# Expert rows moved by id, and a ring slot reloaded in two parts, in a two-layer decoder step

## The reference

```python
def hierarchical_moe(h, rg_w, rg_b, re_w, re_b, w_gate, w_up, w_down):
    x = h.reshape(-1, d)
    gp, gidx = lax.top_k(softmax(x @ rg_w + rg_b), 1)          # one of 4 groups
    sel = take_along_axis((x @ re_w + re_b).reshape(-1, 4, 8), gidx)
    ew, eidx = lax.top_k(softmax(sel), 2)                      # two of its 8 experts
    hid = silu(einsum("nd,edf->nef", x, w_gate)) * einsum("nd,edf->nef", x, w_up)
    out = einsum("nef,efd->nd", hid * gate[:, :, None], w_down)
```

## Time and profile before

| what | value |
|---|---|
| device time, median of 3 runs | 1407.9 us (1406.41 to 1408.34) |
| device time of the profiled execution | 1405.64 us |
| its span, first to last instruction | 1403.9 us |
| PE busy | 1036.7 us, 74% |
| DVE busy | 695.8 us, 50% |
| ACT busy | 326.8 us, 23% |
| POOL busy | 227.7 us, 16% |
| moved by DMA | 305.14 MB, mean 217 GB/s |

### The profile page before, as it was taken

One profiled execution on the slowest core, in us unless ns is written; L12 is line 12 of the kernel. 1 busy time (PEld: TensorE's weight loads), 2 busy tenths in 40 slices (PEclk: granted clock), 3 DMA queues, 4 the chain that ended last, 5 costly groups with the idle time before them and its releaser, 6 DMA issues.

```text
span 1403.9 us, 17270 instructions
## 1 busy us (share of the span) xinstructions
PE 1036.7 (74%) x5203; PEld 631.5 (45%) x5203; DVE 695.8 (50%) x1284; ACT 326.8 (23%) x430; POOL 227.7 (16%) x215
## 2 busy tenths in 40 slices
PE   5999999917767777742769999369927777799850
PEld 4999974413222222221668998235423222233320
DVE  2323324352333333339299999934452333355438
ACT  2222110004333332232210110040004322243330
POOL 3333310020000000022337645000020000000020
PEclk8999999958899998875789999679957989899985
DMA  9475220295999999971130110000195999999943
GB/s 307 142 291 206 76 93 0 80 373 199 388 395 393 398 385 373 382 244 52 59 120 1 61 58 34 7 4 0 55 380 177 391 397 391 389 359 367 371 157 138
DMA packets 78220, 305.14 MB, mean 217 GB/s; under 512 B 13243, under 2 KB 31727, under 8 KB 53583
## 3 DMA queue, kind: packets, MB, share of 16 engines
q1 hardware_dynamic: 56248, 235.16, 44.5%
q10 hardware_dynamic: 16295, 49.76, 10.3%
q0 software_dynamic: 5632, 19.63, 3.9%
HBM read 270.76 MB, written 46.27 MB: 226 GB/s over the span
## 4 chain that ended last, share of the span: by engine, by line
PE 36%; DMA 26%; DVE 23%; issue 5%; SPq 5%; ACT 2%; POOL 2%; ACTq 1%; DVEq 0%; PEldq 0%
DMA ring<-in_moe_w_down_dram 23%; DVE ring L1486 13%; PE ps L881 13%; PE ps L901 10%; PE ps L972 6%; PE ps L987 3%; SPq L408 2%; DMA ring<-in_sc_w_in_dram 1%; POOL rows_sorted L837 1%; PE ps L913 1%; PE ps L958 1%; DVE bn L1172 1%; DVE h L1182 1%; DVE h L1390 1%; DVE h L1392 1%
## 5 line engine op out<-in xcount | busy, mean ns | idle before, releaser
L972 PE MATMUL ps<-arena 128*64 128x512 f32 x1152 | 287.7, 657 | 95.6 <-DVE arena L1349 93.2
L972 PEld LDWEIGHTS ps<-arena 128*64 128x64 f32 x1152 | 88.7, 151 | 291.8 <-issue 161.7
L1486 DVE SCALAR_TENSOR_TENSOR ring<-arena,cvec,ring 128x528 f32<-128x528 f32 x360 | 189.5, 605 | 0.0
L1348 DVE COPY arena<-ring 128x1024 f32 x144 | 99.4, 690 | 168.6 <-SPq L474 146.0
L881 PE MATMUL ps<-hT_hi,w_hi 128*128 128x296 f32 x640 | 145.0, 308 | 33.3 <-POOL w_lo L801 12.6
L901 PE MATMUL ps<-ring 128*128 128x512 f32 (+1 forms) x320 | 140.4, 598 | 11.9 <-ACT ring L750 11.9
L987 PE MATMUL ps<-arena 128*64 128x512 f32 x576 | 131.5, 598 | 21.2 <-DVE arena L1365 21.2
L801 POOL TENSOR_TENSOR w_lo<-ring,w_hi 128x512 fp32r<-128x512 f32 x80 | 109.5, 1371 | 203.8 <-ACT w_hi L538 203.8
L881 PE MATMUL ps<-hT_lo,w_hi 128*128 128x296 f32 x640 | 141.0, 302 | 0.0
L881 PE MATMUL ps<-hT_hi,w_lo 128*128 128x296 f32 x640 | 140.7, 301 | 0.0
L881 PEld LDWEIGHTS ps<-hT_hi,w_hi 128*128 128x128 f32 x640 | 105.0, 192 | 40.9 <-issue 30.0
(11 more groups left out here) (194 smaller groups left out, 962.7 us busy)
## 6 DMA issues: line engine op xcount, KB each, us to landing
ring<-in_moe_w_gate_dram SPq DMA_DIRECT2D x64, 1024.0 KB, 10.2
ring<-in_moe_w_up_dram SPq DMA_DIRECT2D x64, 1024.0 KB, 12.6
ring<-in_moe_w_down_dram SPq DMA_DIRECT2D x64, 1024.0 KB, 14.8
arena<-rows_sorted ACTq DMA_DIRECT2D x160, 128.0 KB
rows_sorted<-arena ACTq DMA_DIRECT2D x144, 128.0 KB
rows_sorted<-stage ACTq DMA_DIRECT2D x27, 512.0 KB, 3.6
ring<-in_sc_w_in_dram SPq DMA_DIRECT2D x12, 1024.0 KB, 12.7
ring<-in_cf_w_pw_dram SPq DMA_DIRECT2D x4, 1536.0 KB, 15.1
```

The costliest lines, as they stand in the source:

```text
L972: ins = nc.tensor.matmul(ps[own, B_GU, :], xT_e[:, k, own], w_gu[:, x, c, i * 2 * F:(i + 1) * 2 * F], start=(k == 0), stop=(k == C - 1))
L1348: nc.vector.tensor_copy(as_gu(w_gu[:, 0, c, :]), gu_chunk(ranks[0], c))
L1486: ins = nc.vector.scalar_tensor_tensor(out=out, in0=src, scalar=cf_tap(k, j), in1=out, op0=ALU.mult, op1=ALU.add)
```

## The change

Rows no longer pass through a sorted array. As each tile of `h` leaves the first LayerNorm, ACT stores it to `x_dram`, in the order of the rows. `route` makes, from the places, the inverse table: with one-hot matrices of each pair's place (its low 7 bits in `r_low`, its duo in `r_high` times the pair's number) PE adds up which pair sits at each place (`ids_turned`), and DVE makes of it the row numbers to gather (`xidx`) and the pair numbers to scatter to (`yidx`); an empty place gets a number beyond the bound, which the DMA leaves out. For each duo POOL then gathers 128 places' rows from `x_dram` and scatters 128 results to `y_dram` with one indirect DMA each. `y_dram` is in the order of the pairs, so that ACT can fetch a tile's two results per row with one plain DMA; `picked` has a buffer for each of the five tiles. The zero fill, the ten scatters, the ten gathers, the pieces and their flags in `tab` go. ACT's down copies of duo 0 come first in its part, before it waits for any row. The last duo stands outside the loops of PE and ACT.

SP waits for `gu_ready` alone before the gate and up DMAs, and for `dn_ready` before the down DMA; it reads the expert's number ahead of both waits.

```diff
-            def load_expert(layer, r, number=None):
+            def load_expert(layer, r, number=None, duos=None):
...
+                down = w_down[layer, e1].rearrange("e (p k) d -> p (e k d)", k=FK)
+                if duos is not None:
+                    sp.wait_ge(gu_ready[layer], NCH * duos + 1)
...
-                                 (s[:, 2 * u:3 * u], w_down[layer, e1].rearrange("e (p k) d -> p (e k d)", k=FK))):
+                                 (s[:, 2 * u:3 * u], down)):
+                    if duos is not None and src is down:
+                        sp.wait_ge(dn_ready[layer], FK * duos + 1)
                     sp.dma_start(dst, src, **cond).then_inc(slot_loaded[r % SLOTS], 16)
...
-                        wait_copied(layer, upto)
-                        load_expert(layer, r, g * SLOTS + r)
+                        load_expert(layer, r, g * SLOTS + r, (upto + 1) // 2)
...
-                def body(s, first=False):
+                def body(s, first=False, final=False):
-                    rank_a, rank_b, y_a, y_b, x_a, x_b = record(mybir.EngineType.Activation, s, 0, 6)
-                    copy_dn(s, (rank_a, rank_b), first)
                     if not first:
-                        store_y(s - 1, (y_a, y_b))
+                        copy_dn(s, record(mybir.EngineType.Activation, s), first)
                     act.wait_ge(gu_used[l], NCH * s + NCH)
...
-                    copy_xT(s + 1)
-                    load_x(s + 2, (x_a, x_b))
+                    if not final:
+                        copy_xT(s + 1)
 
                 act.sem_inc(dn_ready[l], 1)
-                act.wait_ge(scattered, 16 * 2 * NT * (l + 1))
...
-                load_x(0, flags[0:2])
-                copy_xT(0)
-                load_x(1, flags[2:4])
+                copy_dn(0, record(mybir.EngineType.Activation, 0), True)
+                act.wait_ge(x_stored, 16 * NT * (l + 1))
                 for t in range(2):
                     scale_h(t, h_scaled)
+                copy_xT(0)
                 body(0, first=True)
-                with act.Fori(1, last + 1) as s:
-                    body(s)
-                store_y(last, record(mybir.EngineType.Activation, last + 1, 2, 2))
                 for t in range(2, NT):
                     scale_h(t, h_scaled)
-                act.wait_ge(x_loaded[l], (last + 3) * MOVED)
-                act.wait_ge(y_stored[l], (last + 1) * MOVED)
...
+                with act.Fori(1, last) as s:
+                    body(s)
+                body(last, final=True)
+                act.wait_ge(y_stored[l], (last + 1) * 16)
+                for t in range(NT):
+                    n = ROWS[t]
+                    act.dma_start(picked[t][0:n, :], y_dram[2 * t * P:2 * (t * P + n), :].rearrange("(p c) d -> p (c d)", c=2)
+                                  ).then_inc(y_fetched[t], 16)
...
-                if p.index >= 3:
-                    store_blanks(p.index - 3)
...
                     if t >= 1:
                         copy_hT((i + 1) * NT + t - 1)
+                        act.wait_ge(ln_done, i * NT + t)
+                        n = ROWS[t - 1]
+                        act.dma_start(x_dram[(t - 1) * P:(t - 1) * P + n, :], h[0:n, t - 1, :]).then_inc(x_stored, 16)
...
+            def experts(l):
+                pool.wait_ge(tab_ready, l + 1)
+                last = last_duo(pool)
+                x_bound, y_bound = pool.to_reg(T - 1), pool.to_reg(PAIRS - 1)
+                def at_column(i, column, s):
+                    nc.gpsimd.tensor_copy(now[:, i:i + 1], column[:, bass.ds(s, 1)])
+                    pool.drain()
+                    return bass.IndirectOffsetOnAxis(ap=now[:, i:i + 1], axis=0)
+                def load_x(s):
+                    pool.indirect_dma_start(x_rows, None, x_dram[:], at_column(0, xidx, s), bounds_check=x_bound,
+                                            oob_is_err=False).then_inc(x_loaded[l], 16)
+                def store_y(s):
+                    pool.wait_ge(y_copied[l], s + 1)
+                    pool.indirect_dma_start(y_dram[:], at_column(1, yidx, s), y_rows, None, bounds_check=y_bound,
+                                            oob_is_err=False).then_inc(y_stored[l], 16)
+                pool.wait_ge(x_stored, 16 * NT * (l + 1))
+                load_x(0)
+                pool.wait_ge(x_turned[l], 1)
+                load_x(1)
+                with pool.Fori(0, last - 1) as s:
+                    pool.wait_ge(x_turned[l], s + 2)
+                    load_x(s + 2)
+                    store_y(s)
+                store_y(last - 1)
+                store_y(last)
...
-                pool.wait_ge(pos_ready, layer + 1)
...
-                pool.wait_ge(ys_complete, layer + 1)
...
+                experts(layer)
...
+                pe.wait_ge(places_ready, layer + 1)
+                for i in range(2 * NT):
+                    last = nc.tensor.matmul(ps[:, B_IDS, 0:NDUO], r_low[:, i, :], r_high[:, i, :],
+                                            start=(i == 0), stop=(i == 2 * NT - 1))
+                last.then_inc(ids_turned, 1)
...
+                nc.vector.tensor_scalar(posh[:, 0], posi[:], P - 1, None, ALU.bitwise_and)
+                step(nc.vector.tensor_scalar(posh[:, 1], posi[:], P.bit_length() - 1, 1, ALU.logical_shift_right,
+                                             ALU.logical_shift_left))
+                step(nc.vector.tensor_copy(poshf[:], posh[:]))
+                step(tt(r_high, evens[:].unsqueeze(1).to_broadcast([P, 2 * NT, NDUO]),
+                        poshf[:, 1].unsqueeze(2).to_broadcast([P, 2 * NT, NDUO]), ALU.is_equal))
+                step(tt(r_high, r_high, ids[:].rearrange("p c t -> p (c t)").unsqueeze(2).to_broadcast([P, 2 * NT, NDUO]),
+                        ALU.mult))
+                tt(r_low, iota_n[:].unsqueeze(1).to_broadcast([P, 2 * NT, P]),
+                   poshf[:, 0].unsqueeze(2).to_broadcast([P, 2 * NT, P]), ALU.is_equal).then_inc(places_ready, 1)
...
-                nc.vector.memset(x_rows, 0.0)
...
+                dve.wait_ge(ids_turned, layer + 1)
+                found = ps[:, B_IDS, 0:NDUO]
+                step(nc.vector.tensor_scalar(idt[:], found, 0.5, blank[:, 0:1], ALU.is_lt, ALU.mult))
+                step(nc.vector.scalar_tensor_tensor(out=yidx[:], in0=found, scalar=-1.0, in1=idt[:], op0=ALU.add, op1=ALU.add))
+                nc.vector.tensor_scalar(xidx[:], yidx[:], 1, None, ALU.logical_shift_right).then_inc(ids_ready, 1)
```

More of the change, by code:

```diff
@@ L51, in build_decoder_step @@
     NDUO = -(-TILES // 2)
-    XROWS = (NDUO + 2) * P
     CAP = -(-T // R)
@@ L189, in build_decoder_step @@
         hidT = hidT.rearrange("p (k n) -> p k n", k=FK)
-        picked = [v[:, 2 * D * b:2 * D * (b + 1)].rearrange("p (k d) -> p k d", k=2)
-                  for v in (mixT[:].rearrange("p c t -> p (c t)"), work) for b in range(2)]
-        NB = len(picked)
+        tail = ring[:, SHARED * SLOT:SHARED * SLOT + 6 * D]
+        picked = [tail[:, 2 * D * b:2 * D * (b + 1)] for b in range(3)] + [work[:, 2 * D * b:2 * D * (b + 1)] for b in range(2)]
+        assert len(picked) == NT and C * T + DIAGS * P + C * SB >= 6 * D
         r_e = work[:, 0:6 * NT * EG].rearrange("p (i t e) -> p i t e", t=NT, e=EG)
@@ L277, in build_decoder_step @@
         y_stored = [sem(f"y_stored{l}") for l in L]
-        ys_complete = sem("ys_complete")
-        gathered = [sem(f"gathered{b}") for b in range(NB)]
+        y_fetched = [sem(f"y_fetched{t}") for t in range(NT)]
         combined = sem("combined")
         out_stored = sem("out_stored")
-        assert 2 * (3 * C - 3) >= XROWS // P
         NWIN, NWOUT = C // WIN_BLOCKS, 2
@@ L562, in experts @@
                 last = last_duo(act)
-                def move(flags, signal, pieces):
-                    for i, (dst, src) in enumerate(pieces):
-                        cond = dict(cond=flags[i // 2] > 0) if i % 2 else {}
-                        act.dma_start(dst, src, **cond).then_inc(signal, 16)
-                def load_x(s, flags):
-                    move(flags, x_loaded[l], [(x_rows[a:b], rows[bass.ds(s * P + a, b - a), :]) for a, b in PIECES])
-                def store_y(s, flags):
-                    act.wait_ge(y_copied[l], s + 1)
-                    move(flags, y_stored[l], [(rows[bass.ds(s * P + a, b - a), :], y_rows[a:b]) for a, b in PIECES])
                 def copy_xT(s):
@@ L795, in _ @@
             pool.dma_start(harows, state_a[0].rearrange("s r d -> (s r) d")).then_inc(rows_loaded, 16)
+            step(nc.gpsimd.iota(ids[:].bitcast(I32), pattern=[[1, 2], [2 * P, NT]], base=1, channel_multiplier=2))
+            step(nc.gpsimd.tensor_copy(ids[:], ids[:].bitcast(I32)))
+            for c in range(2):
+                nc.gpsimd.tensor_tensor(ids[:, c], ids[:, c], valid[:], ALU.mult).then_inc(iota_made, 1)
             def split_lo(layer, p):
@@ L1004, in experts @@
                 down(0, True)
-                with pe.Fori(1, last + 1) as s:
```

(4 more changed lines are left out.)

120 lines of the change are left out of this document (49 added, 71 removed).

## The result

| | before | after |
|---|---|---|
| median of 15 runs each, alternating | 1408.84 us | 1415.55 us |
| lowest and highest | 1405.09, 1412.37 | 1410.48, 1422.33 |
| ratio | | 1.0046, 95% interval 1.0032 to 1.006 |
| span of the profiled execution | 1403.9 us | 1413.7 us |

The change makes the kernel 0.46% slower. Forecast were 1360 us, with a range from 1342 to 1383.

What follows compares the result with a forecast made beforehand. It took each layer as a stream of 28 expert loads, limited by the DMA engines, that begins late. Start 30, row bytes 15 and split 3 us: 1405.6 - 48 + 2.3 = 1360 us, range 1342 to 1383.

Steps and rivals of the forecast that it cites:

- Costed at nothing: Zero fill, stores to `x_dram`, POOL's index tables, gathers in the loop and the end of a layer: taken as 0 us.
- The slower rival: Duo loops: rows come late in every duo, one gather and one buffer; 1429 us at a 16 us gather, chance 0.05.
- The start: Start of each layer's experts: first reload 17.7 us earlier, stream of loads ahead by 15 us, 30 us over both layers.
- The gap: DMA engines idle between the landing of the first two reloads and the third reload, 332 to 334.5 us in layer 0.
- POOL behind the copies: Rival: POOL must wait until DVE's eight copies end, 5.5 us, at layer starts and in tight duos; 1377 us, chance 0.12.
- the sign that the prediction named: The rival with POOL waiting behind DVE's copies falls if POOL's gathers last about 1 us.
- The bytes of the rows: Duos where DMA sets the pace, 24 of 36: 5.8 MB fewer row bytes at 390 GB/s save 15 us.
- More than forecast: Rival: no gap in the stream of loads and all row bytes counted, 64 us gained; 1344 us, chance 0.08.
- the start that does not move: Rival: something else holds each layer's first reload, so 30 us are missing; 1390 us, chance 0.04.
- the rows that are free: Rival: row bytes gone between weight packets bring nothing; 1375 us, chance 0.13.
- The split: Late in layer 1, where PE sets the pace: gate and up reloads no longer wait for down copies, 3 us gained.
- The end of a layer: From last copy to first combining: a scatter and a fetch replace DVE's 10.73 us wait, no change, 2 us either way.

## Why the prediction was wrong, point by point

- **The step that failed** is in "Costed at nothing": "The gather of duo s+2 starts when duo s+1 is turned and has 12.55 - 1.2 = 11.4 us in the tightest stretch against 6.6; behind it on POOL stands only `store_y`". It does not start then. The drain between its column and itself was costed with the column, "under 1 us", which holds only when nothing is in flight. In most of the loop it waits 6.6 to 9.1 us for the scatter, and the scatter as long for the gather. Without the two drains the gathers land in 8.3 us, longer than the 5.6 taken but within the 11.4, and the time is 1342.
- **The slower rival** had the place right, one duo's rows and one buffer, and the point from which it decides, 16.1 us a duo. It looked for a gather of 15 us; it was a gather and a scatter of some 8.3 each in a row, 18.3 us where this binds. Layer 1 went to 300.7 / 18 = 16.7 us a duo in the mean, not 18.3, so 1416 and not more. Its chance of 0.05 was too low: the drain stands in the diff, and what is in flight when it comes was not asked.
- **The start** was right: first reload 313.62 (forecast 314.5), third 334.41 (334.5), first product 316.61 (316.7), although the table came at 306.0 and not 304.2, since PE's added products took 4.46 us and not 2.4. That the moments fit so closely is in part luck: POOL's first column copy starts 1.0 us behind the table (307.00), where 3.5 were taken, and DVE's first copy 2.4 (308.37). Without the drains the silu of duo 3 comes 19.3 us earlier than before (362.22, 381.52). The gap was a little larger than taken: by the shares of 2 us each, the DMA engines of the changed kernel idle 3.9 us from 330 to 338, not 2.5.
- **POOL behind the copies** did not come true: without the drains POOL's gathers last 1.01 to 1.13 us each, the sign that the prediction named, and PE's wait for rows is 13.6 us, as at the start alone.
- **The bytes of the rows** were a term too small, and for a wrong reason. 15 us were bytes at 390 GB/s. Measured, new rows cost about 1 us a MB in the mean, and the old ones cost more than bytes by where their loads landed. From the silu of duo 4 to that of duo 14 the drainless kernel takes 168.2 us against 180.2, 1.2 a duo, twice the 15 / 24 forecast.
- **The 18 us beyond the forecast**, by the same silus: layer 0 gains 33.7 us where the terms gave 24.4, layer 1 28.5 where they gave 23.6, and the end 1.5, together 15.6 more; the rest is the median against the profiled execution. Of layer 0's 9.3, 5.7 lie between duos 4 and 14, where the only term was that of the rows. Ahead of duo 4 lie 3.6 in layer 0 and 5.7 in layer 1, where the start and the rows mix; they were not taken apart.
- **The other rivals.** *More than forecast*, 1344, is about what the kernel without drains reached, though not for the reasons given there; the start that does not move and the rows that are free fell with the first reload and with the rows above.
- **The split**, 3 us, stays open between 0 and 10.
- **The end of a layer** was right: the first combining waited 9.39 us, against 10.73.

## What to carry to other kernels

A drain on the engine that issues indirect DMAs orders more than that engine's own instructions: here it waited until the transfer in flight had landed, so order a table write before the DMA that reads it with a semaphore on the write. Cost a drain by what is still under way when it comes, and look for two that stand behind each other's transfers. And where weights stream at the engines' limit, look at the rate and not at the busy share, and try small loads spread across all partitions before loads into a block of neighbours.

## What the runs showed of the hardware

- With a drain between, POOL's next indirect DMA went about 0.8 us behind the landing of the one before: 3.3 us to landing and 4.10 from DMA to DMA for the scatters, 8.48 and 9.29 for a gather in the loop. Without one, POOL issues the next indirect DMA 0.30 us behind the end of the last.
- Loads of 32 rows of 4 KB into 32 neighbouring partitions held the whole stream at 264 to 340 GB/s while they ran, beside 422 without them; 49 us for 36 duos with four such loads each, against the same loads spread over the partitions. Stores from such blocks cost nothing that was measured (1399.26 us against 1399.59 with the stores spread as well).
- The busy share of the DMA engines read 1.02 at 380, 394 and 422 GB/s alike.
